# A gated delta rule on one core: the query-key gram first and in other banks, the diagonal of the seed written ahead, the rest of the seed on every second column

## The reference

```python
def gated_delta_chunked(q, k, v, log_g, beta, s0):       # chunks of 64 tokens
    gam = jnp.cumsum(log_g, axis=-1)
    diff = gam[..., :, None] - gam[..., None, :]
    dec_incl = masked_exp(diff, incl)
    dec_strict = jnp.where(strict, dec_incl, 0.0)
    kb = k * beta[..., None]
    m = jnp.einsum('bhnid,bhnjd->bhnij', kb, k) * dec_strict
    a = m + jnp.eye(CHUNK, dtype=q.dtype)
    u = triangular_solve(a, v * beta[..., None], lower=True, unit_diagonal=True)
    w = triangular_solve(a, kb * jnp.exp(gam)[..., None], lower=True, unit_diagonal=True)
    qk = jnp.einsum('bhnid,bhnjd->bhnij', q, k) * dec_incl
    q_dec, g_last = q * jnp.exp(gam)[..., None], jnp.exp(gam[..., -1])
    k_dec = k * jnp.exp(gam[..., -1:] - gam)[..., None]
    def step(s, xs):
        u_c, w_c, qk_c, qd_c, kd_c, gl_c = xs
        v_new = u_c - w_c @ s
        o = qd_c @ s + qk_c @ v_new
        s = gl_c * s + kd_c.T @ v_new
        return s, o
```

## Time and profile before

| | us |
|---|---|
| median of 3 runs | 3590.14 |
| lowest, highest | 3588.86, 3591.29 |
| the profiled execution | 3596.22 |
| its span | 3594.40 |
| the delta rule's steps in it (first product to the last block of matmuls) | 1088.24 to 1575.98 |
| TensorE busy in 1250 to 1350 | 96.20 of 100, granted clock 1.00 |
| VectorE, ScalarE, GpSimd busy there | 79.01, 47.48, 67.19 |

### The profile page before, as it was taken

How to read it: one execution, slowest core, us unless ns; L and a number is a source line. 1 busy time by engine, 2 the same in 40 slices (tenths; PEclk the granted TensorE clock), 3 DMA queues, 4 the chain that set the end, 5 groups by cost and what they waited for, 6 DMA issues and landing times. The chain is left out here.

```text
span 3594.4 us, 114080 instructions
## 1 busy us (share of the span) xinstructions
PE 3215.8 (89%) x48685; PEld 2718.2 (76%) x48685; DVE 2005.1 (56%) x3221; ACT 1530.5 (43%) x2345; POOL 1712.3 (48%) x1366
## 2 busy tenths in 40 slices
PE   6799999999987999976666649999999999999998
PEld 3677788888876999975665548778878878787877
DVE  5488620121006777757776675655565565757575
ACT  5466522333213444424454226654454552323243
POOL 0302333332005666627775285456646657556564
PEclk8899999999999999989899779999999999999999
DMA  5133442344233444444333656765565575646453
GB/s 209 51 62 80 90 97 94 108 128 139 75 101 101 144 144 145 148 126 129 109 108 100 226 205 214 249 189 203 199 223 190 194 275 185 240 163 235 182 213 122
DMA packets 458243, 556.57 MB, mean 155 GB/s; under 512 B 120980, under 2 KB 384504, under 8 KB 433528
## 3 DMA queue, kind: packets, MB, share of 16 engines
q1 hardware_dynamic: 431408, 513.19, 44.7%
q10 hardware_dynamic: 20968, 23.28, 1.9%
q0 software_dynamic: 5632, 16.78, 1.5%
HBM read 355.21 MB, written 197.97 MB: 154 GB/s over the span
## 5 line engine op out<-in xcount | busy, mean ns | idle before, releaser
L3212 PE MATMUL o_pg<-o_t_hi,o_s_hi 128*128 128x512 f32 x2016 | 793.8, 394 | 59.5 <-DVE o_s_lo L3419 22.8
L3214 PE MATMUL o_pg<-o_t_lo,o_s_hi 128*128 128x512 f32 x2016 | 789.9, 392 | 0.0
L3215 PE MATMUL o_pg<-o_t_hi,o_s_lo 128*128 128x512 f32 x2016 | 789.8, 392 | 0.0
L601 PE MATMUL p_pg<-h_hi,p_whi 128*128 128x512 f32 (+1 forms) x1384 | 531.7, 384 | 9.5 <-DVE p_wlo L828 9.5
L601 PE MATMUL p_pg<-h_lo,p_whi 128*128 128x512 f32 (+1 forms) x1384 | 519.4, 375 | 0.0
L601 PE MATMUL p_pg<-h_hi,p_wlo 128*128 128x512 f32 (+1 forms) x1384 | 519.3, 375 | 0.0
L3212 PEld LDWEIGHTS o_pg<-o_t_hi,o_s_hi 128*128 128x128 f32 x2016 | 381.8, 189 | 149.2 <-DVE o_s_lo L3419 46.4
L3215 PEld LDWEIGHTS o_pg<-o_t_hi,o_s_lo 128*128 128x128 f32 x2016 | 381.7, 189 | 80.9
L3214 PEld LDWEIGHTS o_pg<-o_t_lo,o_s_hi 128*128 128x128 f32 x2016 | 382.0, 189 | 78.5
L3419 DVE TENSOR_TENSOR o_s_lo<-o_raw,o_s_hi 128x512 fp32r<-128x512 f32 x288 | 269.4, 937 | 199.1 <-ACT o_s_hi L3248 198.9
L601 PEld LDWEIGHTS p_pg<-h_hi,p_whi 128*128 128x128 f32 x1384 | 262.4, 190 | 61.1 <-DVE p_wlo L828 9.8
(11 more groups left out here) (353 smaller groups left out, 6431.7 us busy)
## 6 DMA issues: line engine op xcount, KB each, us to landing
o_raw<-in_w_mlp SPq DMA_DIRECT2D x32, 1024.0 KB, 5.9
scr_f<-o_xf SPq DMA_DIRECT2D x64, 512.0 KB, 7.7
o_raw<-scr_f SPq DMA_DIRECT2D x32, 1024.0 KB, 5.4
scr_w<-o_pre SPq DMA_DIRECT2D x16, 1792.0 KB, 6.7
o_t_raw<-scr_w SPq DMA_DIRECT2D x28, 1024.0 KB, 5.8
o_xf<-scr_x SPq DMA_DIRECT2D x22, 1024.0 KB, 7.6
p_raw<-in_w_in SPq DMA_DIRECT2D x38, 512.0 KB, 5.8
g_kqa<-scr_kqv SPq DMA_DIRECT2D x72, 256.0 KB, 2.9
```

The source lines that it names most:

```text
L601: last = nc.tensor.matmul(pg[0:m, bank, 0:n], w[:, q, k, 0:m], h[bank][:, k, :], start=(k == 0 and j == 0), stop=(k == KT - 1 and j == 2))
L3212: nc.tensor.matmul(out, s_hi[:, q, k, :], t_hi[:, q, k, :], start=(not more and k == 0), stop=False, skip_group_check=more)
L3214: nc.tensor.matmul(out, s_hi[:, q, k, :], t_lo[:, q, k, :], start=False, stop=False, skip_group_check=more)
L3215: last = nc.tensor.matmul(out, s_lo[:, q, k, :], t_hi[:, q, k, :], start=False, stop=(k == 3), skip_group_check=more)
```

## The change

Five edits, all in `phase_gdn`.

1. TensorE: `gram` does the query-key product first, into `pc` side 0 in place of `pa` side 1, and this half no longer waits for the copies out of `pa`; it waits for the previous `am`. The key-key product follows, into `pa`. The order of the blocks behind `tz` changes. `handed_grown` also waits for the `am` that is read out of `pc`.
2. POOL: the diagonal is written into `tt` itself (`diagonals`), when `tt` has been handed on, by one product with beta; `c2` and the sum on POOL go. `gaps` waits for it. `c1` and `c1e` are formed only for the columns that have an element off the diagonal: the odd ones in the forward half, the even ones in the backward half.
3. VectorE: `decay` makes `seed` from every second column of the gram (two operations, one for each direction), then `nn`, then adds `seed` to every second column of `tt` (two operations). `attend` comes before `decay`, `late_block(4)` before `carried`, and `state` before `handed_block`.
4. TensorE's loop runs over 34 chunks, and the last chunk's body is written out behind it without the gram.
5. `kdvn` is moved ahead and waits for `vn`.

```diff
-        dd, ee, ei, c1, c1e, c2 = (sb("g_" + n, [P, *W]) for n in ("dd", "ee", "ei", "c1", "c1e", "c2"))
+        dd, ee, ei = (sb("g_" + n, [P, *W]) for n in ("dd", "ee", "ei"))
+        c1, c1e, seed = (sb("g_" + n, [P, 2, PAIRS, CH // 2]) for n in ("c1", "c1e", "seed"))
...
                 def gram(i, n):
                     pe.wait_ge(kqa_in, at(i, n, 32, 32))
                     if i is not None or n:
+                        pe.wait_ge(am_ready, at(i, n, 1, 0))
+                    pe.sem_inc(go, 1)
+                    to_tokens(side(pc, 0), chan(kqa, 0), chan(kqa, 1)).then_inc(kq_done, 1)
+                    if i is not None or n:
                         pe.wait_ge(tx_ready, at(i, n, 3, 0))
                         pe.wait_ge(tx_rest, at(i, n, 3, 0))
                     pe.sem_inc(go, 1)
-                    to_tokens(side(pa, 0), chan(kqa, 0), chan(kqa, 0))
-                    to_tokens(side(pa, 1), chan(kqa, 0), chan(kqa, 1)).then_inc(kkq_done, 1)
+                    to_tokens(side(pa, 0), chan(kqa, 0), chan(kqa, 0)).then_inc(kkq_done, 1)
...
-                with pe.Fori(0, NCH - 1) as i:
+                with pe.Fori(0, NCH - 2) as i:
                     body(i, 1, True, True, True)
+                body(None, NCH - 1, True, True, False)
                 body(None, NCH, False, True, False)
...
             def _(pool):
                 def gaps(i, n):
+                    if i is not None or n:
+                        pool.wait_ge(tt_pre, at(i, n, 1, 0))
...
                 def seeds(i, n):
-                    nc.gpsimd.tensor_tensor(c2[:, :, :, :], wide(K_EYE), col(cola[:, Q_BETA]), ALU.mult).then_inc(c_ready, 1)
-                    nc.gpsimd.tensor_tensor(c1[:, :, :, :], wide(K_L1T), col(cola[:, Q_CN]), ALU.mult).then_inc(c_half, 1)
+                    if i is not None or n:
+                        pool.wait_ge(c1e_ready, at(i, n, 1, 0))
+                    for g in range(2):
+                        own = slot(K_L1T)[:, g * CH + 1 - g:(g + 1) * CH:2].unsqueeze(1).to_broadcast([P, PAIRS, CH // 2])
+                        last = nc.gpsimd.tensor_tensor(c1[:, g], own, cola[:, Q_CN, g].unsqueeze(2).to_broadcast([P, PAIRS, CH // 2]),
+                                                       ALU.mult)
+                    last.then_inc(c_half, 1)
+
+                def diagonals(i, n):
+                    if i is not None or n:
+                        pool.wait_ge(tx_done, at(i, n, 3, 0))
+                        pool.wait_ge(tt2_ready, at(i, n, 1, 0))
+                    eye = slot(K_EYE)[:, 0:CH].unsqueeze(1).unsqueeze(1).to_broadcast([P, 2, PAIRS, CH])
+                    beta = cola[:, Q_BETA].rearrange("p g (w y) -> p y (g w)", y=2).unsqueeze(3).to_broadcast([P, 2, PAIRS, CH])
+                    nc.gpsimd.tensor_tensor(tt[:, :, :, :], eye, beta, ALU.mult).then_inc(tt_pre, 1)
...
                 def decay(i, n):
-                    dve.wait_ge(exp_ready, at(i, n, 1, 1))
                     dve.wait_ge(kkq_done, at(i, n, 1, 1))
                     dve.wait_ge(c1e_ready, at(i, n, 1, 1))
-                    if i is not None or n:
-                        dve.wait_ge(tt2_ready, at(i, n, 1, 0))
-                    dve.tensor_tensor(tt[:, :, :, :], pa[:, :, 0], heads_first(c1e), ALU.mult).then_inc(tt_half, 1)
+                    for g in range(2):
+                        last = dve.tensor_tensor(own_heads(seed, g), odd_heads(pa[:, :, 0], g), own_heads(c1e, g), ALU.mult)
+                    last.then_inc(tt_half, 1)
+                    dve.wait_ge(exp_ready, at(i, n, 1, 1))
                     if i is not None or n:
                         dve.wait_ge(nn2_ready, at(i, n, 1, 0))
                     dve.tensor_tensor(heads_first(nn), pa[:, :, 0], heads_first(ee), ALU.mult).then_inc(nn_ready, 1)
+                    dve.wait_ge(tt_half, at(i, n, 1, 1))
+                    dve.wait_ge(tt_pre, at(i, n, 1, 1))
+                    for g in range(2):
+                        last = dve.tensor_tensor(odd_heads(tt, g), odd_heads(tt, g), own_heads(seed, g), ALU.add)
+                    last.then_inc(tt_init, 1)
```

More of the change, by code:

```diff
@@ L1355, in handed_grown @@
                             pe.wait_ge(pred2_done, at(i, m, 3, 3))
+                        if pre:
+                            pe.wait_ge(am_ready, at(i, n, 1, 2))
                         pe.sem_inc(go, 1)
@@ L1389, in kdvn @@
                     def kdvn():
+                        pe.wait_ge(vn_ready, at(i, m, 1, 1))
                         pe.wait_ge(o1_ready, at(i, m, 1, 1))
@@ L1435, in body @@
                     if a:
-                        handed_grown()
+                        turn_keys()
+                    if c:
+                        kdvn()
+                    if a:
                         turn_values()
@@ L1556, in masked @@
                     pool.wait_ge(exp_ready, at(i, n, 1, 1))
-                    nc.gpsimd.tensor_tensor(c1e[:, :, :, :], c1[:, :, :, :], ee[:, :, :, :], ALU.mult).then_inc(c1e_ready, 1)
+                    for g in range(2):
+                        last = nc.gpsimd.tensor_tensor(c1e[:, g], c1[:, g], odd(ee, g), ALU.mult)
+                    last.then_inc(c1e_ready, 1)
                     if i is not None or n:
@@ L1576, in first @@
                     masked(None, 0)
+                    diagonals(None, 0)
                     pool.wait_ge(prep_a, 2)
@@ L1595, in body @@
                         masked(i, n + 1)
+                        diagonals(i, n + 1)
                     if a:
@@ L1617, in decay @@
                     dve.tensor_tensor(heads_first(nn), pa[:, :, 0], heads_first(ee), ALU.mult).then_inc(nn_ready, 1)
+                    dve.wait_ge(tt_half, at(i, n, 1, 1))
+                    dve.wait_ge(tt_pre, at(i, n, 1, 1))
+                    for g in range(2):
+                        last = dve.tensor_tensor(odd_heads(tt, g), odd_heads(tt, g), own_heads(seed, g), ALU.add)
+                    last.then_inc(tt_init, 1)
                 def attend(i, n):
                     dve.wait_ge(ei_ready, at(i, n, 1, 1))
+                    dve.wait_ge(kq_done, at(i, n, 1, 1))
                     if i is not None or n > 1:
                         dve.wait_ge(amb_ready, at(i, n, 1, -1))
-                    dve.tensor_tensor(heads_first(am[n % 2]), pa[:, :, 1], heads_first(ei), ALU.mult).then_inc(am_ready, 1)
+                    dve.tensor_tensor(heads_first(am[n % 2]), pc[:, :, 0], heads_first(ei), ALU.mult).then_inc(am_ready, 1)
                 def first():
@@ L1732, in body @@
                     if c:
+                        late_block(4)
                         carried()
-                        late_block(4)
                     if a:
@@ L1741, in body @@
                     if pre:
+                        attend(i, n + 1)
                         decay(i, n + 1)
-                        attend(i, n + 1)
+                    if c:
+                        state()
                     if a:
@@ L1746, in body @@
                     if c:
-                        state()
                         output()
```

23 lines of the change are left out of this document (11 added, 12 removed).

## The result

| | before | after |
|---|---|---|
| median of the runs, us | 3591.99 (14 runs) | 3598.45 (14 runs) |
| ratio, 95% interval | | 1.0018 [1.0009, 1.0026] |
| profiled execution, us | 3596.22 | 3597.43 |

The change makes the kernel 6.5 us slower by the medians, 0.18%. The forecast was 3580.4, with 3572 to 3595. Of the rivals it is late kvb (3597.5) whose wait stands in the trace.

A forecast was written before the change was run, and what follows sets the result against it. TensorE was taken as nearly full, at a period of 12.665 us. 32 periods at 12.14 gave -17.0, the straight copy +7.3: -9.7 from the median 3590.14, so 3580.4; own range 3575 to 3586, whole range 3572 to 3595.

The forecast's parts named there:

- late kvb: Rival in SP's load queue: kvb lands 1.46 late, stall 0.73, period 12.67, only the copy's 7.3 stays: 3597.5; chance 0.14.
- kvb's lateness: Forecast step in SP's queue: kvb 0.2 to 0.8 late for turning the keys; 0.2 us a chunk taken, period 12.14.
- the rival's 14.85: Late kvb's landing after tz: issue at 10.55, 0.6 to the second half, 3.7 for it to land; chance 0.14.
- the prediction's own sign of being wrong: Stated test: wrong if the period is not below 12.4 or the one straight-copied chunk takes less than 15 us.
- Half of the lateness remained: Steady state of kvb's stall: it also moves the next tz, so half the lateness remains, 0.1 to 0.4 us a chunk.
- TensorE's floor: TensorE's period if nothing waits: 12.665 less 0.67 (wait before the product) and 0.06 (late block) gives 11.94.
- The straight copy: TensorE's last chunk: stalls for newly met code +8.3, gram left out -0.97, together +7.3 us; bounds 0 to +11.
- The first two periods: Start of the stage: the first chunk starts from other waits (VectorE's scans), so nothing was counted.
- POOL's wait gone: TensorE before the chunk's first product: the wait for POOL's seed sum, 0.50 us each, goes; 0.67 us a chunk gained.
- VectorE in time: VectorE's path to the product ends 3.73 after tz, hidden by 0.13 behind TensorE's 3.86.
- a pair of short operations: VectorE's 128-column operations on every second column: 0.50 us a pair taken; the dear price was 0.74.
- the diagonal at 1.05 on POOL: POOL's diagonal of 512 columns: 1.04 us, from 1.50 to 2.54 after tz, needed at 3.09, so hidden.

The follow-up runs named there:

- e1: Kernel after with SyncE's queue reordered to kqa, rows, kvb, store, qb: 3579.86 us, ratio 0.9971 to before.
- e2: Kernel before with only TensorE's loop one chunk shorter and the last chunk written out without the gram: 3597.85 us, ratio 1.0021 to before.
- e3: Kernel after with TensorE's loop over 35 chunks and the last gram, so without the straight copy: 3596.66 us, ratio 1.0021 to before.
- e7: Kernel after with POOL's gaps ahead of the diagonal (beta in its own tile), SP's order as it was: 3575.07 us, ratio 0.9948 to before.
- b1: e7 with TensorE's loop over 35 chunks in place of the straight copy: 3579.63 us, ratio 0.9957 to before.
- e4: Kernel after with SyncE's order kqa, rows, kvb, store, qb and without the straight copy: 3576.44 us, ratio 0.9962 to before.
- e8: Kernel after with SP's order rows, kvb, kqa, store, qb: 3628.25 us, ratio 1.0087 to before.
- e6: Kernel after with SyncE's store of o moved behind kvb only: 3596.23 us, ratio 1.0010 to before.

## Why the prediction was wrong

**The step that failed is kvb's lateness.** Chain and issue times held to 0.3 us: rows at 4.49 after tz, kvb at 10.26. What was mis-sized is its landing. I put kvb in place at 13.55 to 14.15 (0.6 for the second half and a median landing of 3.0) and took a stall of 0.2, near the low end. It was in place at 10.26 + 4.63 = 14.89, within 0.04 of the rival's 14.85. It is needed at 12.08 + 1.43 = 13.5, so it is 1.4 late; the idle time in the rows is 1.2 to 1.3, since a block overlaps the next by 0.2. My reason was that the second issue of a pair finds the first under way. The trace says the opposite. Landings of the two halves in the chunk shown, before (issued at 1286.83) and after (issued at 1280.64):

```profile
DMA to landing us min/median/max: 2.9/2.9/2.9
```

```profile
DMA to landing us min/median/max: 3.3/3.6/3.9
```

After, the first half lands in 3.3 and the second, issued 0.6 later, in 3.9: together 10.26 + 0.6 + 3.9 = 14.76, and 0.1 more until TensorE goes on. The longest landing of 4.4 in the earlier trace rows had been in view. The period of 12.738 is also the prediction's own sign of being wrong, not below 12.4. Against the period without a stall (12.077 in e1) it is 0.66 more, where 0.2 was forecast: 14.8 us over 32 periods.

**Half of the lateness remained, as forecast, but not in the way I thought.** A stalled chunk gives the next its keys in time, for the stall stands behind tz, from which the rows' chain starts. So the full stall comes in every second chunk, with periods of 12.08 and about 13.4 in turn for most of the stage. 15.2 us of waits for kvb took the place of 17.0 us for POOL.

**TensorE's floor was 12.08, not 11.94.** With no stall the product starts 4.09 after tz (1288.02 - 1283.93 in e1), and eight blocks make 3.86. Amvn to the handed block takes 0.55 and the handed block to the product 0.73, though VectorE's sum had ended at 1287.36 there. The loop's branch stands in this last step. Where the loop ends, in the kernel after, the same step takes 0.50 (from 1553.34 to 1553.84), so some 0.23 us belongs to the branch. That the wait for POOL had hidden it before is argued from this, not shown. The higher floor costs 0.14 x 32 = 4.5 us.

**The straight copy costs 14.6 in its stage, not 7.3.** The stalls were forecast (8.3, measured 10.45); what I left out is the clock, which was granted at 0.99 up to the fourth stall and at 0.50 for all that follows it. The loop's first pass, from which I took the price, had run at 1.00 (1114 to 1131) through its own five stalls. With the gram left out, 14.6 - 10.45 + 0.97 = 5.1 us stand beside the stalls, which fits the lower clock. By the Trainium skill (Runtime: NRT & Kernel Launch, section Instruction fetch mechanics) a crossing's cost is mostly hidden; the rows of 1.41 to 3.01 us disagree, as those of the loop's first pass did. In the median the copy costs 7.5 (e2) or nothing that can be told (e3 against after, e7 against b1, e1 against e4), as the next stage gives most of it back. That the place of code matters beyond the stage that changes was in none of my cases.

**The first two periods** took 2.8 more, where I counted nothing. The cause stays open: they take 34.67 (e1) and 37.42 (b1) with kvb in time, 35.20 (e3) and 37.16 (after) with it late. Together with 14.8 for kvb, 4.5 for the floor and 7.3 for the copy, less 0.4 at the start, this makes the 29.0 us between the forecast of 9.7 sooner and the 19.3 later at the stage's end.

**Right were**: POOL's wait gone (from 1150 to 1500 TensorE waits for kvb alone); VectorE in time; a pair of short operations at 0.48 (I took 0.50) and 0.40 from start to start; the diagonal at 1.05 on POOL (1.04); kqa no wait. The Trainium skill's note on cachelines (SBUF — State Buffer, Door 1: The DMA port swizzle) had made the seed dearer, since each element lies in a PSUM line of its own. L1647 reads PSUM at every second column, L1656 SBUF, and both take 0.48 a pair: no such cost shows.

**The chances.** Late kvb had 0.14. It should have had more: it shared its chain with the forecast and was only 0.7 us away from it, less than half of what landings scatter in the earlier trace rows (2.6 to 4.4).

## What to carry to other kernels

Where an operation moves to the end of an engine's loop body, follow everything behind it to the last DMA of the train, and give the transfer that is issued behind others its longest landing, not its median. A load whose chain starts ahead of the place where its lateness stalls can show as a stall in every second chunk only (here 1.4 us late at a period of 12.08); the remedy is to put its issue, or the step that releases its queue, ahead of what need not be early. A straight copy of a loop body in code that keeps TensorE full cost 10 to 16 us here, in stalls and in a lower clock; and a change of code length is to be judged by the whole kernel, since later stages move with it.

## What the runs showed of the hardware

- A pair of 256 KB loads issued directly behind another such pair: a median of 4.1 (e8) to 4.4 us (e6) to landing; the pair in front 2.9.
- Code met for the first time stalled TensorE five times in a body of 22 blocks, 1.41 to 3.01 us each in the kernel after and 0.24 to 3.65 in the six traces with the copy. In the kernel after the granted clock was 0.50 for the 23.2 us from 1572.1 on; in the first pass of the loop before it stayed at 1.00.
- The same 9024 matmuls of HGRN2's stage (rows of the trace) stall for 30 to 38 or for 53 to 64 us, by where their code lies: 32 idle products ahead of it change the one to the other, 16 or 64 don't.
- VectorE's operations of 128 columns on every second column: 0.48 us a pair, products read from PSUM as sums in SBUF.
